# The sums of squares of two attentions by two rounded products instead of one float32 product

## The chip, the cores and the metric

One core of a Trainium2 chip runs the whole program, in one launch. The metric is device time in microseconds (us), the median of several runs. A core has five engines with a queue each, which runs in order: PE (TensorE, the products), DVE (VectorE), ACT (ScalarE), POOL (GpSimd) and SP (which issues most of the transfers). They meet through semaphores alone: an instruction can wait until a semaphore has reached a count, and everything queued behind it on its engine waits with it.

## The reference, cut to what matters

The program is a chain of four transformer layers over 512 tokens of width 1024. Two layers attend: one with a difference of two softmaxes over 8 heads ("attn" here), one with a stick-breaking weight over 16 heads of width 64, taken two at a time ("stick"). Both normalise queries and keys by head, the first also its output:

```
def rms_norm(x, gain):
    xf = x.astype(jnp.float32)
    y = xf * lax.rsqrt(jnp.mean(xf * xf, axis=-1, keepdims=True) + NORM_EPS)
    return (y * gain.astype(jnp.float32)).astype(x.dtype)
...
    q = rms_norm(q.reshape(bsz, seq, C_HEADS, 2, C_HEAD_DIM), q_gain) * (C_HEAD_DIM ** -0.5)
    k = rms_norm(k.reshape(bsz, seq, C_HEADS, 2, C_HEAD_DIM), k_gain)
...
    o = rms_norm(o, sub_gain) * (1.0 - lam_init)
```

and in the stick-breaking layer

```
        z = jnp.einsum('bhqd,bhkd->bhqk', qb, kb) * scale
...
        log_beta = jax.nn.log_sigmoid(z)
        log_one_minus = jnp.where(mask, log_beta - z, 0.0)
        later = lax.cumsum(log_one_minus, axis=3, reverse=True) - log_one_minus
        w = jnp.where(mask, jnp.exp(log_beta + later), 0.0)
        outs.append(jnp.einsum('bhqk,bhkd->bhqd', w, vb))
```

The mean of squares over a head's features is the sum that the change is about.

## The kernel before, in words

**Layout.** Features lie on the 128 partitions, tokens along the free axis, so a sum over features is a product on PE with a matrix of ones (`ones64` for heads of 64, `ones` for 128). Such a product of two float32 operands stands in the trace as two records.

**Dense products.** Weights and activations are split into a rounded high part (`w_hi`, `x_hi`, type float32r) and the rest (`w_lo`, `x_lo`); three rounded products (L2595 to L2597 in the attentions) give nearly float32 accuracy. POOL splits most weights (L556, L563), DVE and ACT the activations.

**Order.** Each engine's program is written out by hand, and the only order between engines is that of the waits. Each attention runs over 8 units `u` (one head with its two halves in attn, two heads in stick) of 4 items `i` (blocks of 128 queries), with `g = 4u + i`. While unit `u` attends, PE computes `q` and `k` of unit `u + 2` in the gaps: `q` is finished in the first half of item 2, `k` in item 3.

**From q to its root.** ACT copies the product out of PSUM (`taken`, L2654) and squares it (`squared`, L2671); PE sums over features (`q_sum` L2624, `k_sum` L2634); ACT takes the reciprocal root (L1859, L1861); DVE scales (`q_normal` L2691, `k_normal` L2696).

**An item of attn**: PE makes the scores (L2764), DVE adds the slope and takes maxima (L2898, L2902), ACT the exponentials (`exps`, L2820), DVE the difference of the two shares (L2937 to L2942), PE turns it (L2794), ACT keeps it in SBUF (L2868, semaphore `at_kept`, which the scores three items later wait for). After four items PE multiplies by the values (`values`, L2774); ACT squares the output (L2826, L2828) and PE sums it (`attn_summed`, L2748).

**An item of stick**: PE makes the scores (L2997); ACT the absolute value, exponential and logarithm two items ahead (`soft`: L3053, L3055, L3060); DVE adds (L3128), runs a scan along the keys (L3133) and closes with two more steps (L3145, L3147, semaphore step `lw`); ACT takes the exponential, which is the weight (L3086); PE turns it (L3029), ACT keeps it (`kept`, L3065), and after four items PE multiplies by the values (L3008). On ACT item 3 is: exponential L3086, the root of `q` of unit `u + 2` (L1859, L1861), two steps of `soft`, then `kept`.

The class `Steps` hands out the counts of a semaphore for named steps.

Of the kernel before, what the change touches and what calls it, by code (L numbers as in the profile page):

```python
# [65 lines left out]

def vector_rows():

    rows, at = [], 0
    index = {}  # L70
    for name, count in [("ln_mix_e", ND), ("ln_mix_o", ND), ("ln_mlp", 2 * ND), ("ln_ple", 2 * ND),
                        ("gmlp_v_gain", 4), ("gdn_out_gain", 1), ("gdn_conv", 48), ("attn_sub_gain", 1),
                        ("attn_q_gain", 1), ("attn_k_gain", 1),
                        ("norm_mix_2", 2 * ND), ("norm_mlp_2", 2 * ND), ("c_2", ND), ("hg_norm_2", 4),
                        ("conv_w_2", 12), ("lb_logits_2", 12), ("q_norm_2", 1), ("k_norm_2", 1),
                        ("ada_b_2", 96)]:
        if at % P + count > P:
            at += P - at % P
        index[name] = at
        rows.append((name, at, count))  # L80
        at += count
    return rows, index, -(-at // P)


def program(nc: bass.Bass, dram, out, upto="end"):
    rows, col, n_tables = vector_rows()
    ctx = ExitStack()
    with ctx:
# [20 lines left out]
        ones64 = sb("ones64", [P, P])  # L109
# [776 lines left out]
        def setup_vector(v):  # L886
# [8 lines left out]
            link(nc.vector.tensor_copy(ident_r[:, :], ident[:, :]))  # L895
            nc.vector.tensor_copy(small[:, 33:34], ones[:, 0:1]).then_inc(consts_ready, 1)
# [1667 lines left out]
        class Front:  # L2564
# [3 lines left out]
            def __init__(self, name, out, q, k, v, nat):  # L2568
                self.out, self.raw = out, name == "attn"
                self.quad, self.q, self.k, self.v, self.nat = name, q, k, v, nat  # L2570
                self.q_summed, self.k_summed, self.v_turned = (sem(f"{name}_{x}") for x in ("q_sum", "k_sum", "v_turn"))
                self.q_rooted = Steps(sem(f"{name}_q_root"), ["sq", "q_ln", "q_rs"])
                self.k_rooted = Steps(sem(f"{name}_k_root"), ["sq", "k_ln", "k_rs"])
                self.v_nat, self.q_n, self.k_n = (sem(f"{name}_{x}") for x in ("v_nat", "q_n", "k_n"))
# [41 lines left out]
            def q_sum(self, pe, w, bank):  # L2616
                if w >= 8:
                    return
                pe.wait_ge(*self.q_rooted.at(w, "sq"))
                if w == 1:  # L2620
                    pe.wait_ge(*freed(*self.chunk("k", 0)))
                if w > 1:
                    pe.wait_ge(self.v_nat, w - 1)
                nc.tensor.matmul(bank[:, :], ones64[:, :], sq[:, 0, :], start=True, stop=True).then_inc(self.q_summed, 1)  # L2624

            def k_sum(self, pe, w, bank, bank_read=None):
                if w >= 8:
                    return
                pe.wait_ge(*self.k_rooted.at(w, "sq"))
# [4 lines left out]
                nc.tensor.matmul(bank[:, :], ones64[:, :], sq[:, 1, :], start=True, stop=True).then_inc(self.k_summed, 1)  # L2634
# [29 lines left out]
            def squared(self, act, x, w):  # L2664
# [6 lines left out]
                nc.scalar.activation(sq[:, c, :], buf, ACT.Square).then_inc(*root("sq"))  # L2671

# [47 lines left out]
        at_small = take([4 * 8])  # L2720

        at_front = Front("attn", "out_o", at_q, at_k, at_v, at_nat)
# [3 lines left out]
        at_mix = Steps(sem("at_mix"), ["o_raw", "o_sq", "o_ln", "o_rs"])  # L2726
# [84 lines left out]
        def attn_scalar(act):  # L2811
# [75 lines left out]
        def attn_vector(v):  # L2887
# [15 lines left out]

            def turned_o(u):
# [23 lines left out]
            full_low(v, 3, 6, at_w)  # L2928
            full_low(v, 3, 7, at_w)
# [3 lines left out]
            for g in range(N_ITEMS):  # L2933
# [38 lines left out]
        st_front = Front("stick", "out_c", st_q, st_k, st_v, st_nat)  # L2972
# [10 lines left out]
        def stick_tensor(pe):  # L2983
# [39 lines left out]
            for g in range(N_ITEMS):  # L3023
                u, i, b, n = rising(g)
                f.parts(pe, u, i, 0)
# [16 lines left out]
                if i == 2:  # L3042
                    f.q_sum(pe, u + 2, ps[1])
# [67 lines left out]
        def stick_vector(v):  # L3111
# [643 lines left out]
```

## Time and profile before

| what | value |
|---|---|
| median of 3 runs | 2647.41 us (2644.93 to 2648.14) |
| profiled execution, its own time | 2644.36 us |
| its span in the trace | 2642.6 us |
| busy PE / DVE / ACT / POOL | 98% / 71% / 48% / 50% |
| attn, from its first sum to its last | 748 to 977 us |
| stick, from its first sum to its last | 2033 to 2218 us |
| one unit of attn / of stick | 26.95 us / 27.27 us |

The profiled execution is its span and 1.76 us around it, and lies 3.05 us below the median of the runs. Busy PE is not PE at its peak, since the ends of its records overlap the next; the distance from the start of one record to the start of the next is what a product costs. A unit's length is the distance of the same record in two neighbouring units.

### The profile page before, as it was taken

Reading aid. Unit: us, or ns where it says so; the run is one execution under the profiler, and the core shown is the slowest. Engines: PE = TensorE matmul, PEld = TensorE weight load, DVE = VectorE, ACT = ScalarE, POOL = GpSimd, SP = SyncE. Lnnn points to the kernel's source line nnn. Section 1 sums busy time; section 2 is a strip of 40 time slices with the busy share of each in tenths; the row PEclk is TensorE's granted clock in tenths of the full one; section 3 lists DMA queues with packets and bytes.
Section 4 is the critical chain, followed back from the end, with each engine's and each line's share of the span. In section 5 each row is a group of like instructions: output and inputs, shape, how many; then the busy total and the mean of one; then the engine's idle time right before and its main releaser. Section 6 shows DMA issues by size and latency. Waiting matters only on the chain.

```text
span 2642.6 us, 38995 instructions
## 1 busy us (share of the span) xinstructions
PE 2596.9 (98%) x14388; PEld 2124.8 (80%) x14388; DVE 1883.9 (71%) x2715; ACT 1277.5 (48%) x2256; POOL 1324.8 (50%) x1720
## 2 busy tenths in 40 slices
PE   9999999999999999999999999999999999999999
PEld 6777788888766678888877888788887666789998
DVE  4766579997576657998844477888875776786664
ACT  4455354444355544444432254455554776455553
POOL 5543543334765555433476866543336555643333
PEclk9999999999999999999999999999999999999999
DMA  5211235554322113555332321255543221233332
GB/s 146 67 49 41 57 120 160 167 162 151 87 64 60 61 58 106 181 170 164 118 115 71 96 64 57 88 168 164 169 138 96 61 60 56 58 102 96 96 96 88
DMA packets 359671, 272.77 MB, mean 103 GB/s; under 512 B 9786, under 2 KB 346052, under 8 KB 359492
## 3 DMA queue, kind: packets, MB, share of 16 engines
q1 hardware_dynamic: 343618, 216.68, 27.8%
q10 hardware_dynamic: 15874, 53.67, 6.0%
q8 instruction: 116, 1.90, 0.3%
q14 instruction: 63, 0.52, 0.1%
HBM read 268.22 MB, written 2.10 MB: 102 GB/s over the span
## 4 chain that ended last, share of the span: by engine, by line
PE 78%; POOL 7%; DVE 6%; issue 5%; ACT 1%; DMA 1%; ACTq 0%; POOLq 0%; DVEq 0%; SPq 0%
PE pair L1378 8%; PE pair L1375 8%; PE pair L1379 8%; POOL w_lo L563 5%; PE ps L1340 4%; PE ps L1343 4%; PE ps L1342 4%; PE ps L2595 3%; PE ps L2597 3%; PE ps L2596 3%; PE pair L1340 3%; PE pair L1343 3%; PE pair L1342 3%; PE ps L653 3%; PE ps L655 2%
## 5 line engine op out<-in xcount | busy, mean ns | idle before, releaser
L632 POOL TENSOR_TENSOR w_lo<-w_raw,w_hi 128x256 fp32r<-128x256 f32 x512 | 485.8, 971 | 754.7 <-ACT w_hi L1457 754.7
L563 POOL TENSOR_TENSOR w_lo<-w_raw,w_hi 128x256 fp32r<-128x256 f32 x588 | 480.2, 847 | 12.3
L1375 PE MATMUL pair<-m_hi,w_hi 128*128 128x512 f32 x1008 | 394.6, 391 | 3.9 <-DVE h L1679 3.9
L1378 PE MATMUL pair<-m_lo,w_hi 128*128 128x512 f32 x1008 | 395.3, 392 | 0.0
L1379 PE MATMUL pair<-m_hi,w_lo 128*128 128x512 f32 x1008 | 394.3, 391 | 0.0
L569 POOL TENSOR_TENSOR slot_mark<-slot_mark 128x1 f32<-128x1 f32 x168 | 44.9, 267 | 517.7 <-PE ps L655 227.4
L653 PE MATMUL ps<-x_hi,w_hi 128*128 128x512 f32 x528 | 223.1, 423 | 4.3 <-DVE x_lo L1147 2.4
L1379 PEld LDWEIGHTS pair<-m_hi,w_lo 128*128 128x128 f32 x1008 | 189.2, 188 | 40.9
L1375 PEld LDWEIGHTS pair<-m_hi,w_hi 128*128 128x128 f32 x1008 | 189.7, 188 | 40.0 <-issue 4.2
L1466 ACT ACTIVATE w_hi<-w_raw 128x512 fp32r<-128x512 f32 x216 | 135.3, 628 | 177.0 <-DVE w_raw L1644 98.2
L1457 ACT ACTIVATE w_hi<-w_raw 128x512 fp32r<-128x512 f32 x256 | 157.6, 624 | 125.6 <-DMA w_raw<-in_w_mlp_dram 46.2
L1378 PEld LDWEIGHTS pair<-m_lo,w_hi 128*128 128x128 f32 x1008 | 189.6, 188 | 33.4
L655 PE MATMUL ps<-x_hi,w_lo 128*128 128x512 f32 x528 | 206.8, 392 | 0.0
L654 PE MATMUL ps<-x_lo,w_hi 128*128 128x512 f32 x528 | 206.2, 391 | 0.0
L556 POOL TENSOR_SCALAR w_hi<-w_raw 128x512 fp32r<-128x512 f32 x294 | 200.1, 698 | 0.0
L1625 DVE TENSOR_TENSOR w_lo<-w_raw,w_hi 128x512 fp32r<-128x512 f32 x216 | 178.0, 835 | 10.9 <-ACT w_hi L1466 10.8
L1679 DVE SCALAR_TENSOR_TENSOR h<-pair,mod,h 128x512 f32<-128x512 f32 x124 | 92.9, 749 | 122.6 <-PE pair L1379 122.5
L2595 PE MATMUL ps<-x_hi,w_hi 128*128 128x512 f32 x336 | 151.6, 451 | 1.5
L1472 ACT ACTIVATE rb<-ps 128x256 f32<-128x256 f32 x156 | 59.8, 383 | 153.0 <-PE ps L1343 152.9
L2597 PE MATMUL ps<-x_hi,w_lo 128*128 128x512 f32 x336 | 131.8, 392 | 0.0
L2596 PE MATMUL ps<-x_lo,w_hi 128*128 128x512 f32 x336 | 131.5, 391 | 0.0
L1679 DVE SCALAR_TENSOR_TENSOR h<-pair,h 128x512 f32<-128x512 f32 x128 | 87.7, 685 | 59.6 <-PE pair L1379 59.2
(522 smaller groups left out, 6987.8 us busy)
## 6 DMA issues: line engine op xcount, KB each, us to landing
w_raw<-in_w_mlp_dram SPq DMA_DIRECT2D x112, 512.0 KB, 5.3
w_raw<-in_mlp_w_dram SPq DMA_DIRECT2D x112, 512.0 KB, 4.9
arena<-in_ada_w_dram ACTq DMA_DIRECT2D x96, 512.0 KB, 4.5
w_raw<-in_w_in_ab_dram SPq DMA_DIRECT2D x28, 512.0 KB, 3.7
w_raw<-in_w_qkv_o_dram SPq DMA_DIRECT2D x24, 512.0 KB, 3.8
w_raw<-in_w_qkv_dram SPq DMA_DIRECT2D x24, 512.0 KB, 3.7
w_raw<-in_w_in_e_dram SPq DMA_DIRECT2D x23, 512.0 KB, 4.0
arena<-in_w_mlp_dram SPq DMA_DIRECT2D x16, 512.0 KB, 5.8
```

The lines of the kernel that those rows point to most:

```text
L556: last = nc.gpsimd.tensor_scalar(w_hi[:, j, k, :], w_raw[:, j, k, :], 1.0, 1.0, ALU.mult, ALU.mult)
L563: last = nc.gpsimd.tensor_tensor(w_lo[:, j, k, :], w_raw[:, j, k, :], w_hi[:, j, k, :].bitcast(F32), ALU.subtract)
L632: last = nc.gpsimd.tensor_tensor(half_slot(w_lo, n)[:, k, :], g_half(hp, c)[:, k, :], half_slot(w_hi, n)[:, k, :].bitcast(F32), ALU.subtract)
L653: nc.tensor.matmul(bank[:, :], w_hi[:, j, k, :], hi[:, k, :], start=(k == 0), stop=False)
L654: nc.tensor.matmul(bank[:, :], w_hi[:, j, k, :], lo[:, k, :], start=False, stop=False)
L655: last = nc.tensor.matmul(bank[:, :], w_lo[:, j, k, :], hi[:, k, :], start=False, stop=(k == ND - 1))
L1375: first = nc.tensor.matmul(bank[:, :], hi[:, t, :], m_hi[:, m, :], start=(t == 0), stop=False)
L1378: nc.tensor.matmul(bank[:, :], hi[:, t, :], m_lo[:, m, :], start=False, stop=False)
L1379: last = nc.tensor.matmul(bank[:, :], lo[:, t, :], m_hi[:, m, :], start=False, stop=(t == 2))
L2595: nc.tensor.matmul(ps[0][:, :], w_hi[:, j, k, :], hi[:, k, :], start=(k == 0), stop=False)
L2596: nc.tensor.matmul(ps[0][:, :], w_hi[:, j, k, :], lo[:, k, :], start=False, stop=False)
L2597: last = nc.tensor.matmul(ps[0][:, :], w_lo[:, j, k, :], hi[:, k, :], start=False, stop=(k == ND - 1))
```

## The change

The squares are split as the dense operands are. ACT makes a rounded copy of them (`hi`), DVE subtracts it from the squares (`square_rest`, the rest, also rounded; step `lo`), and PE sums both parts with rounded ones into the same bank, in two products with float32r operands. This goes for `q` and `k` of all units of both attentions (32 sums) and for the outputs of units 0 to 6 of attn (7); unit 7's output keeps its float32 product. `Chain` replaces `Steps` for these semaphores, with steps `sq`, `hi`, `lo`, and PE now waits for `lo` instead of `sq`. The parts lie in free places (`sq_rest` over `sq`'s own place, `m_hi[:, 7]`, `m_lo[:, 7]`, the end of the arena). In stick the sum of `q` stands three products later in PE's order, inside item 3.

```diff
+class Chain:
...
+    def __init__(self, sem, names, last_names=None, last=None):
+        self.sem, self.names, self.last_names, self.last = sem, list(names), last_names, last
...
+    def at(self, unit, name):
+
+        names = self.last_names if unit == self.last else self.names
+        return self.sem, unit * len(self.names) + names.index(name) + 1
...
+        sq_rest = nc.alloc_sbuf_tensor_at("sq_rest", [P, 2, T], F32R, offset=sq_start)
...
-        ones64 = sb("ones64", [P, P])
+        ones_r = sb("ones_r", [P, P], F32R)
+        ones64 = sb("ones64", [P, P], F32R)
...
+            link(nc.vector.tensor_copy(ones_r[:, :], ones[:, :]))
...
-                self.q_rooted = Steps(sem(f"{name}_q_root"), ["sq", "q_ln", "q_rs"])
-                self.k_rooted = Steps(sem(f"{name}_k_root"), ["sq", "k_ln", "k_rs"])
+                self.q_rooted = Chain(sem(f"{name}_q_root"), ["sq", "hi", "lo", "q_ln", "q_rs"])
+                self.k_rooted = Chain(sem(f"{name}_k_root"), ["sq", "hi", "lo", "k_ln", "k_rs"])
...
-                pe.wait_ge(*self.q_rooted.at(w, "sq"))
+                pe.wait_ge(*self.q_rooted.at(w, "lo"))
...
-                nc.tensor.matmul(bank[:, :], ones64[:, :], sq[:, 0, :], start=True, stop=True).then_inc(self.q_summed, 1)
+                nc.tensor.matmul(bank[:, :], ones64[:, :], self.sq_hi[0], start=True, stop=False)
+                nc.tensor.matmul(bank[:, :], ones64[:, :], sq_rest[:, 0, :], start=False, stop=True).then_inc(self.q_summed, 1)
...
                 nc.scalar.activation(sq[:, c, :], buf, ACT.Square).then_inc(*root("sq"))
+                act.wait_ge(*root.at(w, "sq"))
+                nc.scalar.activation(self.sq_hi[c], sq[:, c, :], ACT.Copy).then_inc(*root("hi"))
+
+            def square_rest(self, v, x, w):
+                if w >= 8:
+                    return
+                root, c = (self.q_rooted, 0) if x == "q" else (self.k_rooted, 1)
+                v.wait_ge(*root.at(w, "hi"))
+                nc.vector.tensor_tensor(sq_rest[:, c, :], sq[:, c, :], self.sq_hi[c].bitcast(F32), ALU.subtract
+                                        ).then_inc(*root("lo"))
...
-            pe.wait_ge(*at_mix.at(u, "o_sq"))
-            nc.tensor.matmul(bank[:, :], ones[:, :], at_sq, start=True, stop=True).then_inc(at_o_summed, 1)
...
+            pe.wait_ge(*at_mix.at(u, "lo"))
+            nc.tensor.matmul(bank[:, :], ones_r[:, :], m_hi[:, 7, :], start=True, stop=False)
+            nc.tensor.matmul(bank[:, :], ones_r[:, :], at_sq_rest[:, :], start=False, stop=True).then_inc(at_o_summed, 1)
...
+                if u < 7:
+                    act.wait_ge(*at_mix.at(u, "o_sq"))
+                    nc.scalar.activation(m_hi[:, 7, :], at_sq, ACT.Copy).then_inc(*at_mix("hi"))
...
             full_low(v, 3, 2, at_w)
+            f.square_rest(v, "q", 0)
             full_low(v, 3, 3, at_w)
+            f.square_rest(v, "k", 0)
...
             full_low(v, 3, 6, at_w)
+            f.square_rest(v, "q", 1)
...
+                if i == 0:
+                    f.square_rest(v, "k", u + 1)
                 maxima(g + 2)
+                if i == 0 and u:
+                    o_square_rest(u - 1)
...
+                if i == 2:
+                    f.square_rest(v, "q", u + 2)
...
-                f.parts(pe, u, i, 0)
+                if i == 3 and u < 6:
+                    f.part(pe, "k", u + 2, range(3, 4))
+                    f.q_sum(pe, u + 2, ps[1])
+                    f.part(pe, "k", u + 2, range(4, 6))
+                else:
+                    f.parts(pe, u, i, 0)
                 pe.wait_ge(st_weight, g + 1)
...
-                if i == 2:
-                    f.q_sum(pe, u + 2, ps[1])
...
+            f.square_rest(v, "q", 0)
+            f.square_rest(v, "k", 0)
             f.q_normal(v, 0, q_gain_s)
             f.k_normal(v, 0, k_gain)
+            f.square_rest(v, "q", 1)
...
+                if i == 0:
+                    f.square_rest(v, "k", u + 1)
...
+                if i == 2:
+                    f.square_rest(v, "q", u + 2)
                 for n_out in out_ends(u, i, 0):
                     add_half(v, "out_c", 0, n_out, gate_col(1, 0, n_out))
```

(The last two groups are stick's DVE program; the first of them stands after the scan of item 0 and ahead of its L3145.)

How the order changes, at three places. First DVE in stick, from the close of item 2 to the close of item 3 of one unit, before:

```order
L3145 TENSOR_TENSOR arena<-pair,arena 128x2x384
L3147 TENSOR_TENSOR arena<-arena,barred 128x2x128
L3128 SCALAR_TENSOR_TENSOR arena<-pair,arena 128x1024
L3133 SCALAR_TENSOR_TENSOR arena<-arena,at_dist 128x512 x2
L3145 TENSOR_TENSOR arena<-pair,arena 128x1024
```

and after, where the lines have moved (L3211 was L3145, L3213 L3147, L3192 L3128, L3197 the scan L3133, and L2704 is the rest of the squares):

```order
L3211 TENSOR_TENSOR arena<-pair,arena 128x2x384
L3213 TENSOR_TENSOR arena<-arena,barred 128x2x128
L2704 TENSOR_TENSOR sq_rest<-sq,m_hi 128x512
L3192 SCALAR_TENSOR_TENSOR arena<-pair,arena 128x1024
L3197 SCALAR_TENSOR_TENSOR arena<-arena,at_dist 128x512 x2
L3211 TENSOR_TENSOR arena<-pair,arena 128x1024
```

The rest of `q`'s squares of unit `u + 2` now stands between item 2 and item 3 of unit `u`; all of item 3's scan is queued behind it. Next ACT in attn, item 2 of a unit, before:

```order
L2654 ACTIVATE arena<-ps 128x512
L2671 ACTIVATE sq<-arena 128x512
L2687 ACTIVATE arena<-ps 128x512
L2820 ACTIVATE arena<-arena 128x128 x2
L2868 ACTIVATE arena<-pair 128x2x128
```

and after (L2678 was L2654, L2695 L2671, L2721 L2687, L2861 L2820 and L2912 L2868; L2697 is the rounded copy):

```order
L2678 ACTIVATE arena<-ps 128x512
L2695 ACTIVATE sq<-arena 128x512
L2697 ACTIVATE at_sq_hi<-sq 128x512
L2721 ACTIVATE arena<-ps 128x512
L2861 ACTIVATE arena<-arena 128x128 x2
L2912 ACTIVATE arena<-pair 128x2x128
```

The copy stands ahead of the exponentials and of `kept`. Last, DVE at the start of attn, before, where L2661 takes a `q` or `k` out of PSUM and L1147 and L1139 split the activations:

```order
L2661 TENSOR_TENSOR arena<-ps,rs 128x512
L1147 SCALAR_TENSOR_TENSOR x_lo<-arena,x_hi 128x512
L1139 SCALAR_TENSOR_TENSOR arena<-h,vt,rs 128x512
L1147 SCALAR_TENSOR_TENSOR x_lo<-arena,x_hi 128x512
L1139 SCALAR_TENSOR_TENSOR arena<-h,vt,rs 128x512
L2691 SCALAR_TENSOR_TENSOR arena<-arena,small,rb 128x512
```

and after (L2685 was L2661, L1168 L1147, L1160 L1139, L2725 L2691):

```order
L2685 TENSOR_TENSOR arena<-ps,rs 128x512
L1168 SCALAR_TENSOR_TENSOR x_lo<-arena,x_hi 128x512
L1160 SCALAR_TENSOR_TENSOR arena<-h,vt,rs 128x512
L2704 TENSOR_TENSOR sq_rest<-sq,at_sq_hi 128x512
L1168 SCALAR_TENSOR_TENSOR x_lo<-arena,x_hi 128x512
L1160 SCALAR_TENSOR_TENSOR arena<-h,vt,rs 128x512
L2704 TENSOR_TENSOR sq_rest<-sq,at_sq_hi 128x512
L2725 SCALAR_TENSOR_TENSOR arena<-arena,small,rb 128x512
```

The first `q`'s rest comes behind one more split of the activations, the first `k`'s behind two.

## Rows read from the trace of the kernel before

**Rows 1.** The page: the span, and PE's busy time, share and instructions.
```profile
span 2642.6 us, 38995 instructions
PE 2596.9 (98%) x14388; PEld 2124.8 (80%) x14388; DVE 1883.9 (71%) x2715; ACT 1277.5 (48%) x2256; POOL 1324.8 (50%) x1720
```

**Rows 2.** Timeline of PE in stick: start, length, engine, line, tiles, count [idle before].
```profile
2092.79 1.12 PE L2624 MATMUL ps<-sq,ones 128*128 128x512 f32 x2
...
2093.98 0.40 PE L2596 MATMUL ps<-x_lo,w_hi 128*128 128x512 f32 x1
...
2101.31 0.50 PE L2595 MATMUL ps<-x_hi,w_hi 128*128 128x512 f32 x1
2101.65 0.40 PE L2596 MATMUL ps<-x_lo,w_hi 128*128 128x512 f32 x1
2101.89 0.39 PE L2597 MATMUL ps<-x_hi,w_lo 128*128 128x512 f32 x1
```

**Rows 3.** Timelines of ACT and PE in attn, item 2 of unit 3.
```profile
860.81 0.63 ACT L2671 ACTIVATE sq<-arena 128x512 f32<-128x512 f32 x1
861.35 0.58 ACT L2687 ACTIVATE arena<-ps 128x512 f32<-128x512 f32 x1
...
862.60 0.37 ACT L2868 ACTIVATE arena<-pair 128x256 f32<-128x256 f32 x1
...
863.17 0.92 PE L2764 MATMUL pair<-arena 64*128 64x384 f32 x4
```

**Rows 4.** Timelines of DVE and PE at the start of attn.
```profile
748.30 1.21 DVE L1139 SCALAR_TENSOR_TENSOR arena<-h,vt,rs 128x512 f32<-128x512 f32 x1
749.43 1.22 DVE L1147 SCALAR_TENSOR_TENSOR x_lo<-arena,x_hi 128x512 fp32r<-128x512 f32 x1
...
748.88 1.02 PE L2634 MATMUL pair<-sq,ones 128*128 128x512 f32 x2
...
767.25 0.66 PE L2794 MATMUL pair<-ident,arena 128*128 128x128 f32 x4 [1.36 <-DVE arena L2942]
```

**Rows 5.** Timeline of DVE in stick, from item 2's close to item 3's.
```profile
2085.84 0.42 DVE L3147 TENSOR_TENSOR arena<-arena,barred 128x256 f32<-128x256 f32 x1
2087.03 1.22 DVE L3128 SCALAR_TENSOR_TENSOR arena<-pair,arena 128x1024 f32<-128x1024 f32 x1 [0.77 <-ACT arena L3060]
...
2091.92 0.81 DVE L3147 TENSOR_TENSOR arena<-arena,barred 128x256 f32<-128x256 f32 x1
```

**Rows 6.** Timelines of ACT and PE in the same unit, items 2 and 3.
```profile
2089.19 0.60 ACT L2654 ACTIVATE arena<-ps 128x512 f32<-128x512 f32 x1 [1.46 <-PE ps L2597]
2089.82 0.63 ACT L2671 ACTIVATE sq<-arena 128x512 f32<-128x512 f32 x1
...
2092.76 1.06 ACT L3086 ACTIVATE arena<-arena 128x1024 f32<-128x1024 f32 x1
2093.95 0.69 ACT L1859 ACTIVATE tt<-ps,small 128x512 f32<-128x512 f32 x1
...
2096.89 1.03 ACT L3065 ACTIVATE arena<-pair 128x1024 f32<-128x1024 f32 x1 [0.44 <-PE pair L3029]
...
2095.82 1.04 PE L3029 MATMUL pair<-ident,arena 128*128 128x128 f32 x8
...
2098.16 2.37 PE L3008 MATMUL ps<-arena 128*64 128x512 f32 x16
```

**Rows 7.** Timelines of DVE, ACT and PE in stick's first unit.
```profile
2043.51 1.02 DVE L3147 TENSOR_TENSOR arena<-arena,barred 128x256 f32<-128x256 f32 x1
...
2046.69 0.64 ACT L2671 ACTIVATE sq<-arena 128x512 f32<-128x512 f32 x1
...
2049.65 0.38 PE L3029 MATMUL pair<-ident,arena 128*128 128x128 f32 x2
```

**Rows 8.** Stretches ahead of stick: window, length, busy time and instructions by engine, clock, DMA.
```profile
1621.10:1624.50 3.40, 1.33 (x8) 1.09 (x8) 3.40 (x7) 0.63 (x1) 1.98 (x2) 1.00 0.04 10
1624.60:1627.90 3.30, 3.30 (x9) 2.62 (x8) 1.14 (x3) 1.26 (x2) 0.00 (x0) 0.50 0.50 146
```

More of the change, by code:

```diff
@@ L64, in before, with __call__ @@
         return self.sem, unit * len(self.names)
+class Chain:
+    def __init__(self, sem, names, last_names=None, last=None):
+        self.sem, self.names, self.last_names, self.last = sem, list(names), last_names, last
+    def __call__(self, name):
+        assert name in self.names
+        return self.sem, 1
+    def at(self, unit, name):
+        names = self.last_names if unit == self.last else self.names
+        return self.sem, unit * len(self.names) + names.index(name) + 1
 def vector_rows():
@@ L103, in program @@
         w_lo = sb("w_lo", [P, 4, ND, P], F32R)
+        sq_start = nc.sbuf_base
         sq = sb("sq", [P, 2, T])
+        sq_rest = nc.alloc_sbuf_tensor_at("sq_rest", [P, 2, T], F32R, offset=sq_start)
         rb = sb("rb", [P, 2, T])
@@ L2564, in program, with __init__ @@
         class Front:
-            def __init__(self, name, out, q, k, v, nat):
+            def __init__(self, name, out, q, k, v, nat, sq_hi):
+                self.sq_hi = sq_hi
                 self.out, self.raw = out, name == "attn"
@@ L2628, in k_sum @@
                     return
-                pe.wait_ge(*self.k_rooted.at(w, "sq"))
+                pe.wait_ge(*self.k_rooted.at(w, "lo"))
                 if w == 1:
@@ L2633, in k_sum @@
                     pe.wait_ge(*bank_read)
-                nc.tensor.matmul(bank[:, :], ones64[:, :], sq[:, 1, :], start=True, stop=True).then_inc(self.k_summed, 1)
+                nc.tensor.matmul(bank[:, :], ones64[:, :], self.sq_hi[1], start=True, stop=False)
+                nc.tensor.matmul(bank[:, :], ones64[:, :], sq_rest[:, 1, :], start=False, stop=True).then_inc(self.k_summed, 1)
             def v_turn(self, pe, w, bank_read):
@@ L2720, in program @@
         at_small = take([4 * 8])
-        at_front = Front("attn", "out_o", at_q, at_k, at_v, at_nat)
+        at_sq_hi = nc.alloc_sbuf_tensor_at("at_sq_hi", [P, 2, T], F32R, offset=arena_start + 4 * 22 * T)
+        at_sq_rest = nc.alloc_sbuf_tensor_at("at_sq_rest", [P, T], F32R, offset=arena_start + 4 * 18 * T)
+        at_front = Front("attn", "out_o", at_q, at_k, at_v, at_nat, [at_sq_hi[:, c, :] for c in range(2)])
         at_z, at_turn, at_pv, at_o_summed = sem("at_z"), sem("at_turn"), sem("at_pv"), sem("at_o_sum")
@@ L2725, in program @@
         at_share = Steps(sem("at_share"), ["inv", "lam", "p0", "diff"])
-        at_mix = Steps(sem("at_mix"), ["o_raw", "o_sq", "o_ln", "o_rs"])
+        at_mix = Chain(sem("at_mix"), ["o_raw", "o_sq", "hi", "lo", "o_ln", "o_rs"], ["o_raw", "o_sq", "o_ln", "o_rs"], 7)
         at_o_t, at_o_hi, at_o_lo = sem("at_o_t"), sem("at_o_hi"), sem("at_o_lo")
@@ L2746, in attn_summed @@
         def attn_summed(pe, u, bank):
-            pe.wait_ge(*at_mix.at(u, "o_sq"))
-            nc.tensor.matmul(bank[:, :], ones[:, :], at_sq, start=True, stop=True).then_inc(at_o_summed, 1)
+            if u == 7:
+                pe.wait_ge(*at_mix.at(u, "o_sq"))
+                nc.tensor.matmul(bank[:, :], ones[:, :], at_sq, start=True, stop=True).then_inc(at_o_summed, 1)
+                return
+            pe.wait_ge(*at_mix.at(u, "lo"))
+            nc.tensor.matmul(bank[:, :], ones_r[:, :], m_hi[:, 7, :], start=True, stop=False)
+            nc.tensor.matmul(bank[:, :], ones_r[:, :], at_sq_rest[:, :], start=False, stop=True).then_inc(at_o_summed, 1)
         def attn_tensor(pe):
@@ L2902, in maxima, with o_square_rest @@
                 nc.vector.tensor_reduce(at_col(g, "max"), sloped, AX_X, ALU.max, negate=True).then_inc(at_max, 1)
+            def o_square_rest(u):
+                v.wait_ge(*at_mix.at(u, "hi"))
+                nc.vector.tensor_tensor(at_sq_rest[:, :], at_sq, m_hi[:, 7, :].bitcast(F32), ALU.subtract
+                                        ).then_inc(*at_mix("lo"))
             def turned_o(u):
@@ L2971, in program @@
         st_w = take([2 * NT, T]).rearrange("p (r k) t -> p r k t", r=2)
-        st_front = Front("stick", "out_c", st_q, st_k, st_v, st_nat)
+        st_front = Front("stick", "out_c", st_q, st_k, st_v, st_nat, [m_hi[:, 7, :], m_lo[:, 7, :]])
         st_z, st_turn, st_pv = sem("st_z"), sem("st_turn"), sem("st_pv")
```

## The prediction

> **What bounds the kernel now.** I read the page first: PE is busy for 98% of 2642.6 us [rows 1], and the timelines of both attentions show PE's records closing up one behind the other, unit after unit, with the same distances. So a product taken from PE shortens the kernel by its own length, as long as nothing that PE waits for becomes later. That second half has to be read from the timelines of ACT and DVE: how long before PE needs it is each thing ready, and what is queued behind the new instructions. The clock view says that PE ran at full rate in both attentions.
>
> **What a sum costs and what it saves.** From the start of a float32 sum to the second product behind it 1.19 us pass (2092.79 to 2093.98) [rows 2]. Two rounded products in a row are 0.24 apart (2101.65 to 2101.89), and the first behind the scores, which are float32, takes 0.34 (2101.31 to 2101.65) [rows 2]. With two rounded products in the sum's place the stretch is 0.34 + 0.23 + 0.23 = 0.80, so a sum is 0.40 shorter. In attn there are 20 of them behind its start (7 of `k`, 6 of `q`, 7 of the output): 8.0 us. In stick 7 of `k`: 2.8 us; the 6 of `q` are inside the chain below. The sums at the two starts are in the terms for the starts.
>
> **What it adds.** 39 copies on ACT and 39 subtractions on DVE. A copy of 128x512 takes what the square takes, 0.63 [rows 3]. A subtraction with both operands in SBUF is not in these stretches as such; the nearest row of its size is the split of an activation, 1.22 [rows 4], which I take as the upper end. One operation of DVE on SBUF alone, L3147, takes 0.42 or 0.81 in the same shape [rows 5], by what POOL does beside it, so the lower end is about half of 1.22, some 0.65. POOL splits weights for most of the time here, so I take 1.1, nearer to the upper. 39 x (0.63 + 1.1) = 67 us of work on engines with half their time free costs nothing by itself; what counts is what stands behind it, place by place.
>
> *Attn, item 2.* When PE has finished `q`, ACT copies, squares, and now rounds, ahead of `v`'s copy, the exponentials and `kept`. In the row, `kept` ends at 862.60 + 0.37 = 862.97 and the scores that wait for it start at 863.17 [rows 3]: 0.20 between them. A hand-over on ACT itself takes 0.03 (2089.19 + 0.60 = 2089.79 to 2089.82 [rows 6]), one between engines some 0.05 by estimate, so 0.15 of it is room. The copy and its own hand-over move L2687, and all behind it, by 0.63 + 0.03 = 0.66. So PE waits 0.66 - 0.15 = 0.5 in units 0 to 5: +3.0 us (bounds 2.4 and 4.2). The other new waits of attn's middle have room: `k`'s and the output's rests fall where DVE waits for scores anyway.
>
> *Attn, start.* The sum of the first `k` starts at 748.88 [rows 4]. DVE reaches the first `q`'s rest at 748.30 + 1.21 = 749.5, then has a rest, a split (1.22), the next activation (about as long or 0.5 shorter) and the second rest to do: 749.5 + 1.1 + 1.0 + 0.7 + 0.7 = 753.0, some 4 us later than PE wants it. PE makes up 0.8 by shorter sums, and some by not waiting for DVE a few us later. But at 767.25 PE waits 1.36 us for DVE before the first turn [rows 4], so there DVE's lateness is PE's. DVE has by then three rests more (3 x 0.65 to 3 x 1.22) and has waited for ACT's rounded copies. I take +3.3, between 2.1 and 5.
>
> *Stick, every unit: the term that decides.* DVE closes item 2 at 2085.84 + 0.42 = 2086.26 and starts item 3's scan at 2087.03, when ACT's logarithm is there [rows 5]. Now `q`'s rest of unit u + 2 stands between the two. PE finishes that `q` only at 2089.19, ACT copies, squares until 2089.82 + 0.63 = 2090.45 [rows 6], and rounds until about 2091.1. The rest then takes DVE to 2092.2, and the scan that started at 2087.03 starts at 2092.25: 5.2 later. The last step of item 3, L3147, starts 4.89 behind it [rows 5], at 2097.15, and takes 0.4 where it had 0.8, as POOL's split is then over: ACT's exponential goes from 2092.76 to 2097.6 [rows 6]. It ends at 2098.7, and PE's turn, at 2095.82 before [rows 6], waits for it. Room was 2.0 us (the exponential ended at 2093.82), 2.9 are left over. But more is queued behind the exponential on ACT: the root of `q` and two steps of the soft part, 2.50 us from 2093.95 to 2096.45 (L3065's start less its idle 0.44) [rows 6], ahead of `kept`. `kept` thus starts at 2098.7 + 2.5 = 2101.1 or 2101.2, ends 1.03 later, and PE's product with the values starts at 2102.2 instead of 2098.16 [rows 6]: +4.0 a unit, with `q`'s shorter sum spent inside. Units 0 to 5 pay it: +24.0. Between the values and the next `q` PE is not held up further: `k`'s rest in item 0 also makes DVE wait for ACT, but item 0 has the smallest scan and its weight is ready long ahead of its turn, and by item 2 DVE is back at `k_normal`, ahead of which it was idle. Bounds: with a rest of 0.65 it is 3.6 a unit, with 1.2 and the late step at 0.8 4.5: 21.6 to 27.
>
> *Stick, start.* `k`'s rest of unit 1 stands ahead of the last two steps of item 0. The squares end at 2046.69 + 0.64 = 2047.33 [rows 7], rounded 2048.0, the rest 2048.9; the last two steps, the second of which took 1.02 and began at 2043.51 before [rows 7], then end at 2050.4, the exponential 0.4 later, and the turn moves from 2049.65 [rows 7] to 2050.9: +1.2 (0.8 to 1.7).
>
> *PE's clock.* Each unit of stick now holds a wait of about 3 us on PE. Elsewhere the trace has a stretch of 3.4 us in which PE was busy for 1.33, and in the next one the granted clock is 0.50, 1.2 GHz instead of 2.4, with 9 products in 3.3 us [rows 8]. Such a stretch costs half its length, 1.7 us, less what falls into the second wait (1.1 us, before the values). I take +2.0 for six units together, between 0 and 10.
>
> **The sum.** -8.0 + 3.0 + 3.3 - 2.8 + 24.0 + 1.2 + 2.0 = +22.7. The span becomes 2665.3, that execution's own time 2667.1. Since that execution lay 3.05 under the median of the runs, I set the forecast for a median of runs at 2647.4 + 22.7 = **2670**.
>
> **Rivals.**
> - *Everything is hidden.* 39 sums x 0.40 = 15.6 us less: 2632. For it: PE is the bound on every page of the profile and both other engines are idle for long. Against it: in stick the wait of DVE for ACT is queued ahead of a chain with 2.0 us of room, and I reckon 4.9; it would have to be over by 2.9 less. 10%.
> - *Only the turn is late in stick.* If ACT could work off the root and the soft part while it waits, PE's loss would be 2.5 to 2.9 a unit: 24.0 becomes 16, and the time 2662. Against it stands ACT's order. 15%.
> - *The clock falls in each of the six units*, and outlasts the second wait: +10 instead of +2, 2678. For it: 3 us are more than the 2.07 (3.40 - 1.33) that PE was not busy ahead of the lower clock in [rows 8]. Against it: PE is busy without a break for all the rest of the unit, and how a pause has to lie for the clock to fall isn't seen here. 12%. The Trainium skill, "TensorE: Matmul & The Clock Gate", section "HAM oscillation — how this bites in real kernels", says that a loop whose every pass holds a pause for data can find the array at its low clock again in every pass. By that rule this rival is the forecast; [rows 8] agrees that a pause can do it.
> - *No change to be seen*, if the stick chain costs 1 us a unit or less and attn gives back what it wins: 2642 to 2653. 5%.
> - My forecast: 58%, with its own range 2663 to 2677.
>
> **How the numbers follow.** A measurement of this kernel can tell 0.2%, 5.3 us, from no change. Faster is the first rival, 10%; the same 5%; slower the rest, 85%. The range leaves out the first and the fourth rival and the upper end of the third: 2655 to 2682.
>
> **What would show it.** In the changed trace's DVE rows of stick, the rest of `q` ahead of the 128x1024 step with an idle time of some 4 us before it that ACT ends, six times; on PE the turn of eight blocks (L3029 before) with about 3 us of idle before it and the values with about 1 us; a unit of 30.9 us where it had 27.27; the units 6 and 7 unchanged. In attn, the scores of item 2 with 0.5 us of idle, a unit of about 26.3 instead of 26.95, and the first turn about 3 us later. The sums at 0.24 a product. The forecast is wrong if DVE's idle time before the 128x1024 step stays near 0.8: then stick gains 5 us and the first rival holds; or if PE's clock shows more than a few stretches of 1.2 GHz.

## The result: 1.0% slower, 2672.6 us

The changed kernel takes 2672.56 us (median of 4 runs, 2671.82 to 2673.16), the kernel before in the same comparison 2646.86 (2644.93 to 2648.14): 25.7 us more, a ratio of 1.0099 with an interval of 1.0087 to 1.0111. The profiled execution of the changed kernel took 2673.16, and its span is 28.8 us longer than that in [rows 1].

From the page of the changed kernel:

```profile
span 2671.4 us, 39074 instructions
...
PE 2598.9 (97%) x14388; PEld 2135.4 (80%) x14388; DVE 1908.0 (71%) x2755; ACT 1299.9 (49%) x2295; POOL 1344.4 (50%) x1720
...
PE 76%; DVE 8%; POOL 7%; issue 5%; ACT 3%; DMA 1%; ACTq 0%; POOLq 0%; DVEq 0%; SPq 0%
```

PE has as many products as in [rows 1] and is busy for only 2 us more, while the span grew by 28.8: most of it went into waiting. (In PE's busy time the shorter sums and products at half the clock, both shown below, work against each other.) The last line, the shares of the chain that ended last, read PE 78%, DVE 6% and ACT 1% before.

**Stick, item 3.** The timeline of the changed kernel in stick's unit 1, all engines (L2678, L2695, L2697 are `q`'s or `k`'s copy, squares and rounded copy, L2704 the rest, L3192 to L3213 DVE's steps of an item, L3147 the exponential, L1880 the first step of the root and L3116 the second step of the soft part, L3092 the turn, L3126 `kept`, L3066 the values):

```profile
2094.52 0.60 ACT L2678 ACTIVATE arena<-ps 128x512 f32<-128x512 f32 x1 [1.45 <-PE ps L2619]
2095.15 0.63 ACT L2695 ACTIVATE sq<-arena 128x512 f32<-128x512 f32 x1
2095.81 0.63 ACT L2697 ACTIVATE m_hi<-sq 128x512 fp32r<-128x512 f32 x1
...
2096.48 0.81 DVE L2704 TENSOR_TENSOR sq_rest<-sq,m_hi 128x512 fp32r<-128x512 f32 x1 [4.93 <-ACT m_hi L2697]
2097.21 1.21 DVE L3192 SCALAR_TENSOR_TENSOR arena<-pair,arena 128x1024 f32<-128x1024 f32 x1
2098.46 2.85 DVE L3197 TENSOR_TENSOR_SCAN arena<-arena,at_dist 128x512 f32<-128x512 f32 x2
2098.92 0.40 PE L2646 MATMUL ps<-m_hi,ones 128*128 128x512 f32 x1
2099.16 0.39 PE L2647 MATMUL ps<-sq_rest,ones 128*128 128x512 f32 x1
...
2102.59 0.42 DVE L3213 TENSOR_TENSOR arena<-arena,barred 128x256 f32<-128x256 f32 x1
...
2103.05 1.06 ACT L3147 ACTIVATE arena<-arena 128x1024 f32<-128x1024 f32 x1 [4.25 <-DVE arena L3213]
2104.01 0.67 ACT L1880 ACTIVATE tt<-ps,small 128x512 f32<-128x512 f32 x1
2104.16 1.97 PE L3092 MATMUL pair<-ident,arena 128*128 128x128 f32 x8 [3.23 <-ACT arena L3147]
...
2105.86 0.63 ACT L3116 ACTIVATE arena<-arena 128x512 f32<-128x512 f32 x1
...
2106.40 1.00 ACT L3126 ACTIVATE arena<-pair 128x1024 f32<-128x1024 f32 x1
...
2108.62 2.99 PE L3066 MATMUL ps<-arena 128*64 128x512 f32 x16
```

In [rows 5] the 128x1024 step waited 0.77 for a logarithm. Now the rest stands ahead of it, DVE idles 4.93 for ACT's rounded copy, and the lateness goes from L3213 to the exponential (idle 4.25) to the turn, ahead of which PE idles 3.23. On ACT the root and two steps of the soft part stand between the exponential and `kept`, as the prediction had it. The sum itself is cheap: its two products start 0.24 apart. The turn, 1.04 long in [rows 6], is 1.97 long, and the values start 1.22 after `kept` has ended (2107.40) without an idle time: PE was still at work, at half its clock.

Stretches of the changed kernel: window, length, busy time (count) of PE, PEld, DVE, ACT and POOL, granted clock, DMA. The first two are stretches of low clock, at unit 0's pause and at that of unit 1 above; the third lies between two of them, the fourth and fifth are the units that begin with the values of units 0 and 1:

```profile
2072.36:2075.77 3.41, 2.88 (x11) 2.69 (x12) 0.49 (x2) 3.35 (x6) 0.00 (x0) 0.50 0.00 0
2103.09:2109.92 6.83, 5.76 (x18) 3.95 (x20) 1.00 (x3) 5.93 (x9) 1.15 (x3) 0.50 0.03 7
2110.00:2130.00 20.00, 19.88 (x101) 14.05 (x97) 12.71 (x18) 13.61 (x21) 11.85 (x17) 1.00 0.19 53
2076.63:2108.62 31.99, 28.64 (x134) 20.12 (x133) 19.44 (x25) 20.98 (x34) 16.55 (x21) 0.91 0.17 50
2108.62:2140.79 32.17, 28.82 (x134) 19.92 (x133) 19.31 (x25) 21.00 (x33) 15.91 (x21) 0.93 0.17 49
```

A unit is 31.4 to 32.2 long where it had 27.27. Every one of the six units has a stretch at 0.50, 1.2 GHz: four of 3.41 us, two of 6.83, each with a pause of 3.23 to 3.25 on PE ahead of it. In the rest of the unit PE is busy and the clock is 1.00.

**Attn.** Timelines of the changed kernel at the start of attn (L2646 and L2657 are the sums of the first `q` and `k`, L2835 the first turn), and in item 2 of unit 0 (L2805 the scores):

```profile
748.41 1.21 DVE L2704 TENSOR_TENSOR sq_rest<-sq,at_sq_hi 128x512 fp32r<-128x512 f32 x1
...
749.67 0.50 PE L2646 MATMUL pair<-at_sq_hi,ones 128*128 128x512 f32 x1 [2.48 <-DVE sq_rest L2704]
...
751.16 1.09 DVE L2704 TENSOR_TENSOR sq_rest<-sq,at_sq_hi 128x512 fp32r<-128x512 f32 x1
...
752.30 0.79 PE L2657 MATMUL pair<-at_sq_hi,ones 128*128 128x512 f32 x1 [1.90 <-DVE sq_rest L2704]
...
757.59 0.63 PE L2618 MATMUL ps<-m_lo,w_hi 128*128 128x512 f32 x1
758.01 0.49 PE L2619 MATMUL ps<-m_hi,w_lo 128*128 128x512 f32 x1
...
772.45 0.33 PE L2835 MATMUL pair<-ident,arena 128*128 128x128 f32 x1 [1.34 <-DVE arena L2994]
...
787.58 0.92 PE L2805 MATMUL pair<-arena 64*128 64x384 f32 x4 [0.46 <-ACT arena L2912]
```

The first `k`'s sum starts 3.4 us later than in [rows 4] and the first turn 5.2. But this execution came to attn earlier than that of before, by 1.0 us, as a product shortly ahead of attn shows, of before first:

```profile
738.89 1.12 PE L1103 MATMUL pair<-rb,ones 128*128 128x512 f32 x2 [1.44 <-DVE rb L1069]
```

```profile
737.87 1.12 PE L1124 MATMUL pair<-rb,ones 128*128 128x512 f32 x2 [1.44 <-DVE rb L1090]
```

Counted from this product, the sum is 4.4 us late and the first turn 6.2. Behind the two pauses the clock is 0.50 from 751.41 to 758.24, and the 14 products there come some 0.43 apart instead of 0.23. From there attn runs as forecast: units of 26.24 to 26.27 us instead of 26.95, with 0.43 to 0.46 of idle ahead of item 2's scores in six units.

### The profile page after: what moved, and what is told of

It is laid out like the page before. It is cut to its first block, busy times and chain, and to the rows that moved or that the text cites. A ratio compares the mean times of both kernels' runs of the same rounds, so it can differ in the third digit from the quotient of the medians.

```text
span 2671.4 us, 39074 instructions
## 1 busy us (share of the span) xinstructions
PE 2598.9 (97%) x14388; PEld 2135.4 (80%) x14388; DVE 1908.0 (71%) x2755; ACT 1299.9 (49%) x2295; POOL 1344.4 (50%) x1720
## 4 chain that ended last, share of the span: by engine, by line
PE 76%; DVE 8%; POOL 7%; issue 5%; ACT 3%; DMA 1%; ACTq 0%; POOLq 0%; DVEq 0%; SPq 0%
PE pair L1399 8%; PE pair L1396 8%; PE pair L1400 8%; POOL w_lo L583 5%; PE ps L1361 4%; PE ps L1364 4%; PE ps L1363 4%; PE pair L1361 3%; PE pair L1364 3%; PE pair L1363 3%; PE ps L2617 3%; PE ps L673 3%; PE ps L2618 2%; PE ps L2619 2%; PE ps L675 2%
## 5 line engine op out<-in xcount | busy, mean ns | idle before, releaser
L652 POOL TENSOR_TENSOR w_lo<-w_raw,w_hi 128x256 fp32r<-128x256 f32 x512 | 487.2, 974 | 752.4 <-ACT w_hi L1478 752.3
L583 POOL TENSOR_TENSOR w_lo<-w_raw,w_hi 128x256 fp32r<-128x256 f32 x588 | 497.2, 876 | 12.3
L673 PE MATMUL ps<-x_hi,w_hi 128*128 128x512 f32 x528 | 223.3, 423 | 4.4 <-DVE x_lo L1168 2.5
L2617 PE MATMUL ps<-x_hi,w_hi 128*128 128x512 f32 x336 | 141.8, 422 | 2.5 <-issue 0.7
```

The source lines that it names most:

```text
L583: last = nc.gpsimd.tensor_tensor(w_lo[:, j, k, :], w_raw[:, j, k, :], w_hi[:, j, k, :].bitcast(F32), ALU.subtract)
L652: last = nc.gpsimd.tensor_tensor(half_slot(w_lo, n)[:, k, :], g_half(hp, c)[:, k, :], half_slot(w_hi, n)[:, k, :].bitcast(F32), ALU.subtract)
L673: nc.tensor.matmul(bank[:, :], w_hi[:, j, k, :], hi[:, k, :], start=(k == 0), stop=False)
L2617: nc.tensor.matmul(ps[0][:, :], w_hi[:, j, k, :], hi[:, k, :], start=(k == 0), stop=False)
```

## The experiments

Ratios are to the kernel before, run on the same chip. A unit is the distance from one unit's values to the next's; stick's are those of units 0 to 5. A single figure holds within 0.04 us.

| kernel | median us (runs) | ratio, interval | attn unit | stick unit |
|---|---|---|---|---|
| changed | 2672.56 (4) | 1.0099 (1.0087 to 1.0111) | 26.24 to 26.27 | 31.4 to 32.2 |
| attn alone | 2649.47 (10) | 1.0007 (0.9997 to 1.0017) | 26.22 to 26.29 | 27.27 |
| stick alone | 2674.19 (4) | 1.0107 (1.0089 to 1.0125) | 26.91 to 26.95 | 31.4 to 32.2 |
| rest behind the scan | 2646.49 (10) | 0.9997 (0.9988 to 1.0007) | 26.27 | 26.92 |
| no rests | 2636.09 (5) | 0.9958 (0.9944 to 0.9972) | 26.25 | 26.51 |
| pause filled | 2667.95 (4) | 1.0076 (1.006 to 1.0092) | 26.22 to 26.27 | 30.87 |
| pause half filled | 2671.85 (4) | 1.0097 (1.0081 to 1.0112) | 26.22 to 26.25 | 30.87 |
| float32 at attn's start | 2640.73 (11) | 0.9974 (0.9965 to 0.9983) | 26.24 | 26.91 |
| `k` and outputs alone | 2639.97 (6) | 0.9968 (0.9955 to 0.998) | 26.15 to 26.19 | 26.88 |
| `q`'s copy on DVE in attn | 2636.11 (5) | 0.9955 (0.994 to 0.9969) | 25.90 | 26.88 |
| rest behind the close | 2639.62 (7) | 0.9966 (0.9955 to 0.9978) | 25.91 to 25.99 | 26.93 |

**Which attention.** In the experiments a function `rounded(x, w)` says which sums are rounded. For stick alone it is, in attn (and for attn alone the same in stick):

```
-  at_front = Front("attn", ..., lambda x, w: True)
+  at_front = Front("attn", ..., lambda x, w: False)
```

> Attn with the rounded sums as in the changed kernel; stick with its float32 sums, without copies and rests, its sum of q in its old place. Theory (the loss is the wait of DVE for q's rounded copy, queued ahead of item 3's scan in stick): attn wins about as much in its units as it loses at its start (0.2 us by the two traces), so 2647, between 2644 and 2650. Rival (the loss is the added work itself, in proportion to the sums): 23 of 39 sums are attn's, so 25.7 x 23/39 = 15 us over before, 2662.

> The counterpart: stick as in the changed kernel, attn with float32 sums throughout. Theory: all of the loss stays, 2671 to 2675. Rival (added work in proportion): 16 of 39 sums, 25.7 x 16/39 = 10.5 us over before, 2657.

The loss is stick's: attn alone is within 0.07% of before, stick alone is as slow as the whole change. The attn that I reckoned at -1.7 us gave nothing to speak of, which leaves something unaccounted at its start.

**What in stick.** One step of DVE's program moves, from the end of item 2 to behind item 3's scan:

```
+                if i == 3:
+                    f.square_rest(v, "q", u + 2)
...
-                if i == 2:
-                    f.square_rest(v, "q", u + 2)
```

> The changed kernel with one line moved in stick: DVE takes the rest of q behind the scan of item 3 (ahead of its last two steps) instead of ahead of item 3. No operation more or less. Theory: the scan ends at about the time the copy is there, so the rest waits some 0.5 us and the weight comes 1.2 to 1.6 us later than in the kernel before, inside its 2.0 us of room; kept comes 0.2 to 0.6 late; PE has no pause of more than 1 us, so its clock stays up. A unit of stick 27.2 to 27.8 us instead of 32.0, the time 2647 to 2652. Rival (the amount of work on DVE and ACT, or the later sum of q on PE): as changed, 2670 to 2675.

The timelines of this kernel in the same unit:

```profile
2088.86 2.34 DVE L3208 TENSOR_TENSOR_SCAN arena<-arena,at_dist 128x512 f32<-128x512 f32 x2
2091.71 1.03 DVE L2713 TENSOR_TENSOR sq_rest<-sq,m_hi 128x512 fp32r<-128x512 f32 x1 [0.51 <-ACT m_hi L2706]
...
2094.15 0.40 PE L2649 MATMUL ps<-m_hi,ones 128*128 128x512 f32 x1
...
2098.78 1.40 PE L3077 MATMUL ps<-arena 128*64 128x512 f32 x6 [0.36 <-ACT arena L3137]
```

The same rest now waits 0.51 instead of 4.93, because the scan runs while ACT rounds, and PE still doesn't wait at the sum. The six pauses ahead of the turn and the stretches at 0.50 in stick are gone; the unit is 26.92. The whole of the 26 us in stick hung on where one subtraction of about 0.8 us stands in DVE's queue. It isn't free in its new place: PE now waits 0.36 ahead of the values, and the unit is 0.41 above that of the next kernel, which has no rests.

> The changed kernel without any rest on DVE: PE waits for the rounded copy and multiplies it twice, so that PE's work and ACT's work are as changed (the sums come out twice as large, the low parts are left out). Theory: with DVE's wait gone the gain on PE shows: attn units of 26.2 to 26.3 us (the copy's 0.5 us at item 2 stays), its start within 1 us of before, stick units 26.5 to 27.0; 2635 to 2642. Rival (ACT's copies are what delays, not DVE's rest): 2655 or more.

```
-  nc.tensor.matmul(bank[:, :], ones64[:, :], sq_rest[:, 0, :], start=False, stop=True)
+  nc.tensor.matmul(bank[:, :], ones64[:, :], self.sq_hi[0], start=False, stop=True)
```

This gives the price of the sums alone: the stick unit is 26.51, 0.76 under 27.27 for two sums, 0.38 each where I took 0.40. The attn unit keeps its 26.25 and its pause of 0.43, so that pause is the copy's on ACT and not the rest's.

**What the clock costs.** PE gets work that changes nothing during the pause:

```
                     f.part(pe, "k", u + 2, range(4, 6))
+                    for _ in range(13):
+                        nc.tensor.matmul(ps[0][:, :], m_lo[:, 6, 0:P], x_hi[:, 0, :], start=False, stop=False)
```

> The changed kernel, and in stick's item 3 of units 0 to 5, right ahead of PE's wait for the weight, 13 rounded products of 128x512 with a weight of zeros, added into the bank of the k that is being made (its value stays). They fill 13 x 0.23 = 3.0 us of the pause of 3.23. Theory (the six pauses are what pulls the clock down, and that costs some 6 us): the pauses shrink to some 0.3 us, the granted clock stays at 1.0 through stick, PE waits about 1 us ahead of the values instead, the unit is 30.9 instead of about 32.0, and the time some 6.5 us under the changed kernel's 2672.6: 2664 to 2668. Rival (the clock is only a mark, and DVE's and ACT's chain sets the unit at 32.0 in any case): units of 31.9 to 32.2, 2671 to 2676. Second rival (the filling products are late themselves and push the turn back): units over 32.3, over 2676.

> As e5_busy_wait, with 7 filling products instead of 13, so that 3.23 - 7 x 0.23 = some 1.6 us of each pause stay in stick's units 0 to 5. Theory 1 (any such pause lets the clock fall in a unit, as the one of 3.23 did): granted clock 0.5 in each unit and units of 31.4 to 32.2, time 2671 to 2674. Theory 2 (it takes a longer pause than that): clock 1.0 through stick, units of 30.86 as in e5, time 2666 to 2669. In either case the pauses themselves cost the same, since DVE and ACT set when the weight is there.

The timeline of PE in the kernel with 13 products (L3099 the filling, L3105 the turn, L3077 the values):

```profile
2100.86 3.11 PE L3099 MATMUL ps<-x_hi,m_lo 128*128 128x512 f32 x13
2104.27 1.09 PE L3105 MATMUL pair<-ident,arena 128*128 128x128 f32 x8 [0.31 <-ACT arena L3160]
...
2107.57 0.65 PE L3077 MATMUL ps<-arena 128*64 128x512 f32 x2 [0.81 <-ACT arena L3139]
```

With the pause filled, the granted clock is 1.0 through all of stick and the unit is 30.87. The changed kernel's units are 31.94 on average (five distances, 2076.63 to 2236.33), so the clock cost 1.07 a unit, 6.4 us for six. (The medians of the two kernels differ by 4.6; by the ratios, each to the kernel before on the same chip, it is 6.1.) So the clock isn't only a mark. What is left, 30.87 - 27.27 = 3.6, is the chain of DVE and ACT, net of the shorter sums, and now PE waits 0.81 ahead of the values.

With 7 products, timeline and stretches of one unit:

```profile
2104.15 1.09 PE L3105 MATMUL pair<-ident,arena 128*128 128x128 f32 x8 [1.67 <-ACT arena L3160]
```

```profile
2076.59:2107.45 30.86, 28.25 (x139) 19.87 (x139) 19.19 (x25) 20.86 (x34) 16.36 (x22) 1.00 0.18 52
```

In this execution, of 2668.08 us, a pause of 1.67 in each unit left the clock at 1.00, as theory 2 has it. The other three took 2670.69 to 2674.67, so that the median is what theory 1 gave; all four with the full filling lie between 2667.52 and 2668.22. Only the 2668.08 execution's trace is at hand, but the mean granted clock was taken in every execution: 0.998, 0.997, 0.998 and 0.997 with half the filling, 0.998 in all four with the full one, 0.993 in all four of the changed kernel. Six stretches of 3.41 us at half the clock would lower the mean by 6 x 3.41 x 0.5 / 2670 = 0.004. So in none of the four did the clock fall in every unit: theory 1 is out, and that the median lies in its range is chance. One or two falls in the two executions at 0.997 would fit; what else made three of them slower is open.

**Attn's start and item 2.** Float32 for `q` and `k` of attn's first two units:

```
-  lambda x, w: True
+  lambda x, w: w > 1
```

> The order of e3_rest_behind_scan in stick, and attn's units 0 and 1 take q and k by the float32 product as before (4 of the 39 sums). Theory (attn's start costs about 5 us by DVE's late rests and the half clock behind the pauses): no pauses of 1.9 to 2.5 us at attn's start, no clock fall there, the values of attn's unit 0 as early as before instead of 4.9 us later, and the time 4 to 5 us under e3's 2646.5: 2641 to 2643. Rival (the start's lateness is taken up by other waits before attn's end): 2645 to 2648.

The timeline of PE at that kernel's start of attn:

```profile
748.26 1.02 PE L2646 MATMUL pair<-sq,ones 128*128 128x512 f32 x2
...
749.12 1.02 PE L2661 MATMUL pair<-sq,ones 128*128 128x512 f32 x2
...
767.50 0.66 PE L2845 MATMUL pair<-ident,arena 128*128 128x128 f32 x4 [1.37 <-DVE arena L3004]
```

The two sums run without a wait and the first turn is 0.25 from [rows 4]'s place. The median is 5.8 below that of the kernel with the rest behind the scan, just under the theory's range (by the ratios, since the two ran on different chips, 6.1). The traces agree: from the product ahead of attn (738.89 before) to the first values 48.81 us pass before and 48.91 here, but 53.5 to 54.7 in the five traces whose start is rounded and has its rests. So the theory holds, and the start's price up to the first values is 4.7 to 5.9 us, not 3.3.

> Only sums that nothing urgent is queued behind are changed: in attn k of units 2 to 7 and the outputs, in stick k of units 2 to 7; all sums of q and of the two starts are the float32 product, stick's order is that of before. 19 sums x 0.40 = 7.6 us. Theory (a sum gives its 0.40 wherever its rest is early): attn unit 26.95 - 0.80 + at most 0.1 = 26.15 to 26.25, stick unit 26.87 for units 0 to 5, no new pause on PE, time 2639 to 2641, ratio 0.997. Rival (the extra 19 copies and rests slow DVE or ACT elsewhere): 2645 to 2649.

> As e7_k_and_o, and attn's q of units 2 to 7 is rounded too, with the rounded copy made by DVE ahead of the rest instead of by ACT, so that kept in item 2 isn't put back by 0.66 us. Theory (the pause of 0.43 us ahead of the scores in item 2 is that copy on ACT): the pause goes, the attn unit is 26.95 - 3 x 0.40 = 25.75 to 25.9, stick unit 26.87, time 2636 to 2638.5, ratio about 0.9962. Rival (two operations of DVE, some 1.7 us, between q's squares and what DVE does next in item 2 make the maxima or the differences late): a new pause ended by DVE, attn unit 26.2 or more, time 2640 or more.

The copy of `q`'s squares, in attn alone, is taken from ACT and given to DVE:

```
+                if self.raw and x == "q":
+                    v.wait_ge(*root.at(w, "sq"))
+                    nc.vector.tensor_copy(self.sq_hi[c], sq[:, c, :]).then_inc(*root("hi"))
```

Both came out as expected. With 19 sums whose rests are early the kernel is 0.3% faster than before. With `q`'s rounded copy on DVE the pause ahead of item 2's scores is gone, and the attn unit is 25.90, 1.05 under 26.95 for three sums. The timeline of DVE and PE in item 2 of unit 0 (L2818 the scores):

```profile
783.11 0.43 DVE L2714 CAST at_sq_hi<-sq 128x512 fp32r<-128x512 f32 x1 [0.39 <-ACT sq L2702]
...
783.57 1.11 DVE L2716 TENSOR_TENSOR sq_rest<-sq,at_sq_hi 128x512 fp32r<-128x512 f32 x1
...
784.81 0.92 PE L2818 MATMUL pair<-arena 64*128 64x384 f32 x4
```

The copy takes 0.43 on DVE (0.63 on ACT) and lies where nobody waits. At 2636.1 this is the fastest kernel that computes all of it.

> Attn as in e8_copy_on_dve; in stick k and q of units 2 to 7 by rounded products, with the sum of q where the changed kernel has it, and DVE's rest of q behind both closing steps of item 3 instead of ahead of its scan (e3_rest_behind_scan had it between the scan and the closing steps, which put the exponential back by 1.0 us and left a pause of 0.36 on PE ahead of the values). PE reaches that sum 1.7 us after e3's rest was done, the closing steps take 1.6, so the rest is just early enough. Theory (only what is queued behind the rest on DVE counts): no pause ahead of the values, stick unit 27.27 - 2 x 0.40 = 26.45 to 26.6 for units 0 to 5, against 26.88 in e8, time 2633 to 2635, ratio about 0.995. Rival (the rest is now late for the sum): a pause ended by DVE at the sum, unit 26.8 to 27.2, time 2636 or more.

```
                 nc.vector.tensor_tensor(buf[:, :, n - P:n], ..., ALU.add).then_inc(*st_item("lw"))
+                if i == 3:
+                    f.square_rest(v, "q", u + 2)
```

Here I was wrong; the rival held. DVE and PE in that kernel's unit 1:

```profile
2090.32 1.22 DVE L2716 TENSOR_TENSOR sq_rest<-sq,m_hi 128x512 fp32r<-128x512 f32 x1
...
2091.59 0.50 PE L2649 MATMUL ps<-m_hi,ones 128*128 128x512 f32 x1 [0.16 <-DVE sq_rest L2716]
...
2095.88 1.40 PE L3080 MATMUL ps<-arena 128*64 128x512 f32 x6
```

The rest took 1.22, where that of the kernel with the rest behind the scan took 1.03, and the closing step ahead of it 0.81 where it took 0.42 there. Nor was the room 1.7: by that kernel's own lines it is 1.4 (2091.71 + 1.03 to 2094.15). So PE, done with its products some 0.3 earlier, waits for the rest: the unit is 26.93, as if `q`'s sum had stayed float32. In stick `q`'s rounded sum pays in none of the three places tried for its rest; 26.51 without rests is what another place could reach.

## Why the forecast came out right

2670 was forecast and 2672.6 measured, inside the forecast's own range of 2663 to 2677. Its deciding step held, two sizes around it were too small, and that the figure lies as near as it does is in part luck.

- **The stick chain, +24.0 for six units.** Right: 4.0 a unit less 0.40 for `k`'s sum makes 30.87, and with the clock held up the unit is 30.87. The inside is not quite as I had it: the rest took 0.81, not 1.1, and the steps from L3192 to L3213 took 5.38 (2097.21 to 2102.59) instead of 4.89; the two nearly cancel. (The step at 2087.03, called the scan there, is L3128 ahead of the scan; the sum is the same.)
- **Only the turn is late**, 2662: refuted. `kept` starts at 2106.40, behind the root and the soft part, and with the clock held up a unit is 3.6 over 27.27, where this rival gives 2.1 to 2.5 once `k`'s shorter sum is taken off.
- **PE's clock, +2.0 between 0 and 10: too small.** It fell in every unit and cost 6.4. The third rival was right about that, and wrong that it adds 10, since part of each stretch lies in the pause itself (2103.09 to 2104.16 above) and over the 0.81 that PE would wait ahead of the values anyway. That is why the 1 us of idle before the values, which I named as a mark, didn't appear in the changed kernel and did with the pause filled. By the rule cited from the Trainium skill, "TensorE: Matmul & The Clock Gate", section "HAM oscillation — how this bites in real kernels", this rival was the forecast; the trace agrees, six units of six. The prediction also gave more than a few stretches of 1.2 GHz as a sign that it is wrong: there are six in stick and one at attn's start, and the trace of before has none in either attention. So on the clock it was wrong by its own sign.
- **Attn's start, +3.3 between 2.1 and 5: too small.** The wait was about as forecast (the first `k`'s sum 4.4 late, for "some 4"). I had not thought of the clock there: 14 products 0.2 us slower are 2.8 us. With the 0.4 that each of the next sums saves taken off, that is about the 6.2 of the first turn. (The prediction's sum to 753.0 counts the split with 1.0 and the second rest with 0.7, where its text names 1.22 and 1.1; the second rest ended at 752.25.)
- **Stick's start, +1.2 between 0.8 and 1.7:** right. From a product shortly ahead of stick (2019.83 before, 2020.63 after) the first turn is 0.9 later. In it is a wait that was not forecast, 0.88 for the rest of the first `k` (2035.76).
- **The sums.** 0.38 a sum instead of 0.40. Attn's units came to -0.69 where the terms give -0.70, three sums less the 0.5 of item 2, which measured 0.43 to 0.46.
- **The sum.** 22.7, and 4.4 more for stick's clock and 2.9 for attn's start, make 30.0; the spans differ by 28.8. By the places of the same products in the two traces that is -1.0 ahead of attn, +1.2 from there to attn's last values (the terms gave -1.7), +0.6 between the attentions and +28.0 from just ahead of stick to the end (the terms gave 24.4, and 4.4 more for the clock). That the medians differ by only 25.7 is because the two profiled executions lie differently to their medians: that of before 2.5 below, that of after 0.6 above. So 2.6 us off the median hides some 7 us by which two terms were too small; with them put right the same way of reckoning gives 2647.4 + 30.0 = 2677, further off than 2670.
- **Everything is hidden**, 2632: the sums alone do give about that (2636.1 without the rests, with the copy's pause in attn's item 2 still in it), and with 25 of the 39 sums rounded where their rests are early 2636.1 was reached as well. What I held against it, the order on DVE, is what cost.

## What to carry to other kernels

A cheap instruction costs what is queued behind it, not its own length: 0.8 us of DVE ahead of a scan, waiting for another engine, made a unit of stick 3.6 us longer than before with the clock held up, and behind the scan the unit was 0.35 shorter than before. When a step is split over two more engines, put each new part where its input is long ready and its engine would wait anyway, and leave the old form where no such place was found (here the starts, and `q` in stick). And price a new pause of PE together with the clock behind it: here that was another 1.1 us a unit on top of 3.6.

## What was not expected of the hardware

- A pause's cost in clock is not a fixed one. Pauses of 3.23 to 3.25 us, alike in length and followed by the same products, were followed by 3.41 us at 1.2 GHz four times and by 6.83 twice in one execution.
- A pause can cost clock in one execution and not in another. In all twelve traces PE pauses for 2.05 to 2.07 us between 1616 and 1626 us (it is the pause in [rows 8]). In ten of them, before and after among them, 3.41 us at 0.50 follow; in those of the kernel without rests and of the float32 start none. One shorter pause, of 1.81 us up to 1061.44 in the kernel with `k` and outputs alone, was followed by 3.41 us at 0.50 as well; the six of 1.67 in the kernel with the half-filled pause were not. Of the float32 start, PE's timeline and the stretch behind it:

```profile
1615.95 1.00 PE L3317 MATMUL pair<-arena 128*128 128x64 f32 x8
1619.01 0.47 PE L1260 MATMUL ps<-m_hi,w_hi 128*128 128x512 f32 x1 [2.06 <-POOL w_lo L582]
```

```profile
1619.10:1622.50 3.40, 3.40 (x19) 2.89 (x19) 2.52 (x6) 1.27 (x2) 0.40 (x2) 1.00 0.53 154
```

- Some of the spread between executions arises before either attention. Near 388 us PE waits for DVE's squares, for 0.95 us in the changed kernel's trace, 2.06 in that of before and 4.14 in that of the kernel with the rest behind the close; in the last of these the clock then fell at 392.31 for 3.41 us, in the first two it didn't. So a span alone can be some 4 us off, and units were compared.
- The same subtraction of 128x512 took 0.69 to 1.22 us, as L3147 did with 0.42 and 0.81. The prediction put the difference down to POOL's splits beside it. For L3147 the trace of before bears that out: all 19 that had nothing on POOL beside them took 0.42 or 0.43, and all nine of 0.68 or more had a split of POOL beside them. For the subtraction it doesn't decide: in the changed kernel 31 of the 32 for `q` and `k` had POOL at work beside them, and among these are some of 0.69 and some of 1.22. What else does is open.
